# A macaron transformer layer on one core: x in four column chunks between the first weight blocks, and ten unread matmuls at the head of TensorE's program

## What is computed

```python
def _rmsnorm(x, g):
    y = xf * lax.rsqrt(jnp.mean(xf * xf, axis=-1, keepdims=True) + EPS)
    return y * g
x = x + 0.5 * _swiglu(_rmsnorm(x, ffn1_norm[l]), w_gate, w_up, w_down)   # D_FF = 5632
```

## Time and profile before

| | us |
|---|---|
| median of three runs | 2510.61 |
| lowest and highest run | 2506.28 and 2514.45 |
| span of the profiled execution | 2504.7 |
| busy in that span: PE, PEld | 2453.5, 2389.8 |
| busy in that span: DVE, ACT, POOL | 1186.1, 801.0, 138.6 |

### The profile page before, as it was taken

One profiled execution on the slowest core, in us unless ns is written; L12 is line 12 of the kernel. 1 busy time (PEld: TensorE's weight loads), 2 busy tenths in 40 slices (PEclk: granted clock), 3 DMA queues, 4 the chain that ended last, 5 costly groups with the idle time before them and its releaser, 6 DMA issues.

```text
span 2504.7 us, 36768 instructions
## 1 busy us (share of the span) xinstructions
PE 2453.5 (98%) x16307; PEld 2389.8 (95%) x16307; DVE 1186.1 (47%) x892; ACT 801.0 (32%) x686; POOL 138.6 (6%) x59
## 2 busy tenths in 40 slices
PE   7999999999999999999999989999999999999998
PEld 5999999999999999989899669999999999999998
DVE  6444444444444447345484226444444444444445
ACT  3322322232323224333333224323322332233223
POOL 2000000000000001000000001000000000000001
PEclk9999999999999999999999899999999999999999
DMA  5444444444444444515153113444444444444441
GB/s 193 152 152 151 151 150 145 145 147 149 150 151 151 151 150 152 162 62 179 55 151 119 42 43 118 152 152 151 150 145 147 146 150 150 151 151 151 151 147 64
DMA packets 178896, 345.98 MB, mean 138 GB/s; under 512 B 10383, under 2 KB 17046, under 8 KB 178518
## 3 DMA queue, kind: packets, MB, share of 16 engines
q1 hardware_dynamic: 175942, 337.11, 41.8%
q0 software_dynamic: 2160, 7.60, 0.9%
q10 hardware_dynamic: 736, 0.41, 0.1%
HBM read 339.45 MB, written 5.65 MB: 138 GB/s over the span
## 4 chain that ended last, share of the span: by engine, by line
PE 95%; DVE 3%; ACT 1%; DMA 0%; issue 0%; SPq 0%; DVEq 0%; ACTq 0%
PE ps L1202 29%; PE ps L1203 29%; PE ps L1204 29%; DVE mov_lo L822 2%; DVE w_lo L805 1%; PE ps L1554 1%; PE ps L1553 1%; PE ps L1383 1%; PE ps L1381 0%; DMA work<-in_x_sample 0%; PE ps L1278 0%; PE ps L1564 0%; PE ps L1412 0%; PE ps L1579 0%; PE ps L1428 0%; PE ps L1238 0%
## 5 line engine op out<-in xcount | busy, mean ns | idle before, releaser
L1202 PE MATMUL ps<-mov_hi,w_hi 128*128 128x320 f32 x3568 | 1108.3, 311 | 9.6 <-DVE w_lo L805 8.6
L1203 PE MATMUL ps<-mov_lo,w_hi 128*128 128x320 f32 x3568 | 1104.4, 310 | 0.0
L1204 PE MATMUL ps<-mov_hi,w_lo 128*128 128x320 f32 x3568 | 1104.2, 309 | 0.0
L805 DVE TENSOR_TENSOR w_lo<-raw,w_hi 128x2048 fp32r<-128x2048 f32 x313 | 717.3, 2292 | 744.7 <-ACT w_hi L499 744.6
L499 ACT CAST w_hi<-raw 128x2048 fp32r<-128x2048 f32 x313 | 596.8, 1907 | 1429.0 <-PE ps L1204 1428.9
L1202 PEld LDWEIGHTS ps<-mov_hi,w_hi 128*128 128x128 f32 x3568 | 671.7, 188 | 12.7 <-issue 10.3
L1203 PEld LDWEIGHTS ps<-mov_lo,w_hi 128*128 128x128 f32 x3568 | 671.6, 188 | 0.5
L1204 PEld LDWEIGHTS ps<-mov_hi,w_lo 128*128 128x128 f32 x3568 | 671.5, 188 | 0.0
L1202 PE MATMUL ps<-h_hi,w_hi 128*128 128x320 f32 x1488 | 462.9, 311 | 4.7 <-DVE h_lo L894 4.7
L1203 PE MATMUL ps<-h_lo,w_hi 128*128 128x320 f32 x1488 | 462.4, 311 | 0.0
L1204 PE MATMUL ps<-h_hi,w_lo 128*128 128x320 f32 x1488 | 462.3, 311 | 0.0
(11 more groups left out here) (193 smaller groups left out, 835.9 us busy)
## 6 DMA issues: line engine op xcount, KB each, us to landing
raw<-in_ffn_w_gate SPq DMA_DIRECT2D x88, 1024.0 KB, 5.2
raw<-in_ffn_w_up SPq DMA_DIRECT2D x88, 1024.0 KB, 5.2
raw<-in_ffn_w_down SPq DMA_DIRECT2D x88, 1024.0 KB, 5.1
raw<-in_w_in SPq DMA_DIRECT2D x28, 1024.0 KB, 5.3
raw<-in_w_out SPq DMA_DIRECT2D x16, 1024.0 KB, 5.1
raw<-in_mla_w_uq SPq DMA_DIRECT2D x12, 256.0 KB, 4.2
raw<-in_w_in SPq DMA_DIRECT2D x4, 640.0 KB, 4.1
work<-in_x_prompt SPq DMA_DIRECT2D x2, 1024.0 KB, 6.4
```

The lines of the kernel that those rows point to most:

```text
L805: dve.tensor_tensor(w_lo[:, n % SPLIT_SLOTS, :], raw[:, n % RAW_SLOTS, :], w_hi[:, n % SPLIT_SLOTS, :].bitcast(F32), ALU.subtract).then_in ...
L1202: pe.matmul(out, w[0], x[0], start=first, stop=False)
L1203: pe.matmul(out, w[0], x[1], start=False, stop=False)
L1204: return pe.matmul(out, w[1], x[0], start=False, stop=last)
```

## The change

SP loads x in four chunks of 512 columns, chunk 0 first, and the others each ahead of one of the gate blocks 1 to 3; gate block 0 comes in four quarters with a semaphore each. The gains are now loaded by ACT's queue and the lambdas by POOL's. PE's program begins with ten matmuls of the tile of ones, whose result nobody reads; then it turns the gains and lambdas, then x tiles 0 to 3, and goes to unit 0. Tiles 4 to 7, 8 to 11 and 12 to 15 are turned in the middle of units 0, 1 and 2. All x tiles go through banks 4 to 7. Unit 0 runs with its four row tiles as the outer loop, each started when its part of `mov_lo` and its quarter of `w_lo` are there.

ACT makes `mov_hi` and DVE `mov_lo` straight from PSUM, and DVE copies the tile to `xT` after that. POOL's squares, the additions and PE's sum for the first block are gone. In their place ACT squares x in its token layout with a running sum along the row (`sum_x`, three instructions), mean, root, reciprocal and the Newton step are made on 128 x 3 elements (`x_norm`), and in the middle of unit 3 PE spreads the factors over the partitions with three matmuls (`spread_rstd`); DVE copies the result to `rstd` (`x_spread_out`). The load of the rest of the table moves behind the first up loads. Semaphore counts of the later norms are renumbered to match.

The diff without new semaphores, renumbered counts and context:

```diff
-        x_in = [sem(f"x_in{i}") for i in range(3)]
+        x_in = [sem(f"x_in{q}") for q in range(4)]
+        first_in = [sem(f"first_in{k}") for k in range(UK - 1)]
...
-            return j if j < 4 else 4 + j % 4
+            return 4 + j % 4
...
-            for t, (r0, rows) in enumerate(TOK):
-                src = x_prompt[0, r0:r0 + rows, :] if t < 2 else x_sample[0]
-                sp.dma_start(wk(X_TOK + t * D, D, slice(0, rows)), src).then_inc(x_in[t], 16)
-            for col, g, n in ((G_F1, ffn1_norm[0], KT), (G_MIX, mix_norm[0], KT), (G_F2, ffn2_norm[0], KT),
-                              (G_FIN, final_norm, KT), (G_SUB, da_subln[0], 1), (G_Q, q_norm[0], 4),
-                              (G_KV, kv_norm[0], 2)):
-                sp.dma_start(wk(S_ROWS, P, slice(col, col + n)),
-                              g.rearrange("(j p) -> j p", p=P)).then_inc(gains_in, 16)
-            for c, v in enumerate((lq1, lq2, lk1, lk2)):
-                sp.dma_start(wk(S_LROWS, HALF, slice(c, c + 1)), v).then_inc(lam_in, 16)
+            def x_load(q):
+                cols = slice(UC * q, UC * q + UC)
+                for t, (r0, rows) in enumerate(TOK):
+                    src = x_prompt[0, r0:r0 + rows, cols] if t < 2 else x_sample[0, :, cols]
+                    sp.dma_start(wk(X_TOK + t * D + UC * q, UC, slice(0, rows)), src).then_inc(x_in[q], 16)
             def ffn_loads(u0, gate, up, down):
+                if u0 == 0:
+                    x_load(0)
+                    for k in range(UK):
+                        sp.dma_start(raw[:, 0, UC * k:UC * k + UC], gate[0, P * k:P * k + P, 0:UC]
+                                     ).then_inc(first_in[k] if k < UK - 1 else raw_in[0], 16)
+                    for q in range(1, 4):
+                        x_load(q)
+                        load(q, 0, block_of(gate, UC * q, 0))
+                else:
+                    for q in range(4):
+                        load(u0 + q, 0, block_of(gate, UC * q, 0))
                 for q in range(4):
-                    load(u0 + q, 0, block_of(gate, UC * q, 0))
+                    load(u0 + 4 + q, 0, block_of(up, UC * q, 0))
                 if u0 == 0:
                     sp.dma_start(tab[:, C_STACK:C_ALL], table[:, C_STACK:C_ALL]).then_inc(tab_in, 16)
-                for q in range(4):
-                    load(u0 + 4 + q, 0, block_of(up, UC * q, 0))
                 with sp.Fori(0, PARTS - 1) as i:
...
             pool.memset(ones[:, :], 1.0).then_inc(ones_set, 1)
+            for c, v in enumerate((lq1, lq2, lk1, lk2)):
+                pool.dma_start(wk(S_LROWS, HALF, slice(c, c + 1)), v).then_inc(lam_in, 16)
...
-            pool.wait_ge(x_copied, 4)
-            pool.tensor_tensor(wk3(F_ACC, 4, T), xT[:, 0:4, :], xT[:, 0:4, :], ALU.mult).then_inc(squared, 1)
-            pool.wait_ge(x_copied, 8)
-            pool.tensor_tensor(wk3(F_SQ, 4, T), xT[:, 4:8, :], xT[:, 4:8, :], ALU.mult).then_inc(squared, 1)
-            add_squares(0)
...
-                    if f == 0 and j < 2:
-                        first_moving_hi(2 + j)
-                        square(0, 2 + j)
+                    if f == 0 and j < 3:
+                        first_moving_hi(j + 1)
+                        sum_x(j)
                     if j == 2:
-                        root(2 * f)
+                        root(2) if f else x_roots()
...
+            for col, g, n in ((G_F1, ffn1_norm[0], KT), (G_MIX, mix_norm[0], KT), (G_F2, ffn2_norm[0], KT),
+                              (G_FIN, final_norm, KT), (G_SUB, da_subln[0], 1), (G_Q, q_norm[0], 4),
+                              (G_KV, kv_norm[0], 2)):
+                act.dma_start(wk(S_ROWS, P, slice(col, col + n)),
+                              g.rearrange("(j p) -> j p", p=P)).then_inc(gains_in, 16)
+            def x_tile_hi(j):
+                act.wait_ge(x_turned, j + 1)
+                act.activation(mov_hi[:, j, :], ps[:, x_bank(j), 0:T], ACT.Copy,
+                               scale=gains[:, G_F1 + j:G_F1 + j + 1]).then_inc(x_hi, 1)
+            def first_moving_hi(q):
+                for j in range(4 * q, 4 * q + 4):
+                    x_tile_hi(j)
+            def sum_x(t):
+                rows = TOK[t][1]
+                if t == 0:
+                    act.wait_ge(tok_set, 1)
+                    for q in range(4):
+                        act.wait_ge(x_in[q], 16 * 3)
+                else:
+                    act.wait_ge(x_sums, t)
+                act.activation(wk(F_SQ, D, slice(0, rows)), wk(X_TOK + t * D, D, slice(0, rows)), ACT.Square,
+                               accum_out=xs[0:rows, t:t + 1]).then_inc(x_sums, 1)
+            def x_roots():
+                act.wait_ge(x_mean, 1)
+                act.activation(xs[:, 3:6], xs[:, 0:3], ACT.Sqrt).then_inc(x_root, 1)
             act.wait_ge(gains_set, 1)
-            def first_moving_hi(q):
-                act.wait_ge(x_copied, 4 * q + 4)
-                moving_hi(0, q, G_F1)
-            first_moving_hi(0)
-            hi(0)
-            first_moving_hi(1)
+            for k in range(UK):
+                x_tile_hi(k)
+                act.wait_ge(first_in[k] if k < UK - 1 else raw_in[0], 16)
+                act.copy(w_hi[:, 0, UC * k:UC * k + UC],
+                         raw[:, 0, UC * k:UC * k + UC]).then_inc(first_hi if k < UK - 1 else hi_done, 1)
...
-                    if f == 0 and j < 2:
-                        moving_lo(0, 2 + j, G_F1)
-                    if f == 0 and j == 0:
-                        copy_x(3)
+                    if f == 0 and j < 3:
+                        x_tiles_lo(j + 1)
                     if j == 2:
-                        norm(2 * f, 4 * ((g0 + 1) % 2))
+                        norm(2, 4 * ((g0 + 1) % 2)) if f else x_norm()
                     if j == 3:
+                        if f == 0:
+                            x_spread_out()
                         drain_gate(u0 + 3, 0, g0)
...
+            dve.memset(xs[:, :], 1.0)
             dve.memset(tok[:, :], 1.0).then_inc(tok_set, 1)
-            def copy_x(q):
+            def x_tile_lo(j):
+                dve.wait_ge(x_hi, j + 1)
+                dve.scalar_tensor_tensor(mov_lo[:, j, :], ps[:, x_bank(j), 0:T], gains[:, G_F1 + j:G_F1 + j + 1],
+                                         mov_hi[:, j, :].bitcast(F32), ALU.mult, ALU.subtract).then_inc(x_lo, 1)
+            def copy_x(j):
+                dve.tensor_copy(xT[:, j, :], ps[:, x_bank(j), 0:T]).then_inc(x_copied, 1)
+            def x_tiles_lo(q):
                 for j in range(4 * q, 4 * q + 4):
-                    dve.wait_ge(x_turned, j + 1)
-                    dve.tensor_copy(xT[:, j, :], ps[:, x_bank(j), 0:T]).then_inc(x_copied, 1)
-            copy_x(0)
+                    x_tile_lo(j)
+                    copy_x(j)
+            def x_norm():
+                dve.wait_ge(x_sums, 3)
+                dve.tensor_scalar(xs[:, 0:3], xs[:, 0:3], 1.0 / D, EPS, ALU.mult, ALU.add).then_inc(x_mean, 1)
+                dve.wait_ge(x_root, 1)
+                y, a, v = xs[:, 3:6], xs[:, 6:9], xs[:, 0:3]
+                link(dve.reciprocal(y, y))
+                link(dve.tensor_tensor(a, y, y, ALU.mult))
+                link(dve.tensor_tensor(a, a, v, ALU.mult))
+                link(dve.tensor_scalar(a, a, -0.5, 1.5, ALU.mult, ALU.add))
+                link(dve.tensor_tensor(a, a, y, ALU.mult))
+                dve.wait_ge(ones_set, 1)
+                for t, (r0, rows) in enumerate(TOK):
+                    last = dve.tensor_scalar(wk(F_ACC + P * t, P, slice(0, rows)), ones[0:rows, :],
+                                             xs[0:rows, 6 + t:7 + t], None, ALU.mult)
+                last.then_inc(x_rstd, 1)
+            def x_spread_out():
+                dve.wait_ge(x_spread, 1)
+                dve.tensor_copy(rstd[:, :], ps[:, 4, 0:T]).then_inc(x_rstd, 1)
+                dve.wait_ge(x_rstd, 2)
             dve.wait_ge(gains_turned, 1)
-            dve.tensor_copy(gains[:, :], ps[:, 7, 0:G_ALL]).then_inc(gains_set, 1)
-            dve.tensor_copy(lamin[:, 0:4], ps[0:HALF, 7, 128:132]).then_inc(gains_set, 1)
-            copy_x(1)
-            moving_lo(0, 0, G_F1)
-            lo(0)
-            copy_x(2)
-            moving_lo(0, 1, G_F1)
+            dve.tensor_copy(gains[:, :], ps[:, 0, 0:G_ALL]).then_inc(gains_set, 1)
+            dve.tensor_copy(lamin[:, 0:4], ps[0:HALF, 0, 128:132]).then_inc(gains_set, 1)
+            dve.wait_ge(gains_set, 1)
+            for k in range(UK):
+                x_tile_lo(k)
+                dve.wait_ge(first_hi if k < UK - 1 else hi_done, k + 1 if k < UK - 1 else 1)
+                cols = slice(UC * k, UC * k + UC)
+                dve.tensor_tensor(w_lo[:, 0, cols], raw[:, 0, cols], w_hi[:, 0, cols].bitcast(F32),
+                                  ALU.subtract).then_inc(first_lo if k < UK - 1 else lo_done, 1)
+            for j in range(4):
+                copy_x(j)
...
```

(71 more changed lines are left out.)

36 lines of the change are left out of this document (20 added, 16 removed).

## The result

The changed kernel took 2491.73 us (median of 11 runs, 2483.86 to 2497.02), the one before 2507.05 (11 runs beside them, 2499.82 to 2518.93): ratio 0.993, interval 0.9913 to 0.9946. The forecast was 2494.7, in a range of 2488 to 2503. The span fell from 2504.7 to 2489.7 us, by 15.0. The time of a run on record is its span and 2.4 to 3.8 us more in the kernel before, 1.9 to 2.2 in the changed one.

What follows compares the result with a forecast made beforehand. TensorE (PE), busy 98% of the span, was taken as the bound, with gain only before unit 4. Its start moving from 64.13 to 48.2 took 15.9 us off span 2504.7, giving 2488.8; plus 5.9, 2494.7 us, range 2488 to 2503.

Steps and rivals of the forecast that it cites:

- Small rows in at 7.0: At the start: gain and lambda loads, on ACT's and POOL's queues, landed by 7.0 us, at the earliest 5.7, latest 11.
- Rival 2: At the start: the small rows land at 11 us, as before the change; time 2498.7 us; chance 10%.
- Unit 0 at 11.3, bound by PE's turn: Unit 0 starts at 11.3 us instead of 29.59, after PE's turns; the ACT and DVE chain ends at 10.7.
- Unit 0 lasts 10.8: Unit 0 takes 10.8 us as before, with a turn and some 13 slow matmuls, ending at 22.1.
- Units 1 and 2 at 9.25, unit 3 at 7.65: Units 1 and 2 hold a turn each, 9.25 us; unit 3 swaps summing for three matmuls, 7.65 us.
- T4 = 48.2: Start of unit 4, the first up-projection unit: 48.2 us in the changed kernel instead of 64.13.
- DVE's chain 0.8 us ahead of PE at unit 1: In unit 0: DVE's splits, tiles and copies end at 21.3 us, 0.8 us before PE is done.
- Rival 3: Units 0 to 2: DVE's chain outlasts PE's unit at the dear tile price, some 3 us thrice; 2503.5 us; chance 8%.
- x all in at 18 to 19, where ACT needs it at 19.1: Last x chunk lands at about 18 to 19 us, when ACT's first row sum comes to it, 19.1.
- Rivals 1 and 5: Units 0 to 3: clock falls in each turn, 2499.5 us, 12%; or stays at 1.2 GHz until unit 4, 2520.8 us, 4%.
- rival 4: Behind the earlier start: something later, such as a wait in the first loop turn, gives it back; no change; chance 6%.
- 5.9 us from span to time: Whole kernel: the runs' median, 2510.61 us, lies 5.9 above the execution's span; carried over to the changed kernel.

Runs made afterwards that it cites:

- e10: The changed kernel again, unaltered, as a check on how well it repeats: 2494.14 us, ratio 0.9937 to the kernel before.
- e7: Changed kernel with a tiny unread activation on ACT ahead of its wait for the gains, loading the function table early: 2487.74 us, single run.
- e1: Changed kernel without its ten dummy matmuls: 2492.49 us, ratio 0.9945 to the kernel before.
- e4: Changed kernel with eleven useless multiplications of a scratch tile on POOL, from the first turned tile on: 2492.15 us, single run.
- e6: Changed kernel with 22 dummy matmuls at the head instead of 10, and ten more behind the first turn: 2484.77 us, single run.
- e8: Changed kernel with the edits of e5, e6 and e7 together: 2489.48 us, single run.
- e11: e8 with step 0's x tiles ahead of block 1's split, row sums one step later, and 16 and 2 dummies: 2489.29 us, ratio 0.9932 to kernel before.
- e3: Kernel before the change, with the squares of x tiles 0 to 7 made by ACT instead of POOL: 2499.54 us, single run.
- e2: Changed kernel with all four x chunks loaded ahead of the first weight block: 2500.64 us, single run.
- e5: Changed kernel with the lambdas turned in unit 3, so PE's start waits for the gains alone: 2494.87 us, single run.

## Why the prediction held, and where it was off

The mechanism was right: the whole change acts up to unit 4, the PE chain is unbroken from unit 0 on, and the sign and the size are about as forecast. Point by point, by the prediction's steps:

- **Chunk 0 near 5 us, the last weight quarter near 8:** the numbers given there (2 us, then 704 and 1728 KB at 418 KB per us) make 3.7 and 6.1. Nothing hung on it: neither PE nor ACT waited for either.
- **Small rows in at 7.0:** 7.46, in e10 6.97. Rival 2 (11 us) is out. That the separate queues are the reason was not tried; the rows landed with the stream at 387 GB/s in the slice from 7 to 8 us.
- **Unit 0 at 11.3, bound by PE's turn:** 12.34, and bound by the other chain, which I had at 10.7. This step failed. I had let ACT load its table as soon as the gains were there. In the trace the load starts at 9.09, when the first turned tile is released; it stands behind that wait. On this chain the load costs 0.9 us, the small rows 0.5 and the first pieces of ACT and DVE 0.3, together the 1.6 from 10.7 to 12.34. e7 moves the load away, which takes 1.3 us off the first `mov_hi` tile.
- **Unit 0 lasts 10.8:** 11.9. The slow beginning had 20 matmuls at 0.27 us, where the kernel before had 12 (I had put it at 13), 1.0 us more. In e1 it had 12, in e10 18; how many it is hangs on when the clock rises, which no step of mine could give.
- **Units 1 and 2 at 9.25, unit 3 at 7.65:** 9.37 twice and 8.0. Together 0.6 us; the summing is six records in 0.81 us where I had 0.54.
- **T4 = 48.2:** 1.0 + 1.1 + 0.2 + 0.4 = 2.7 later; measured 51.02.
- **DVE's chain 0.8 us ahead of PE at unit 1:** its eighth `mov_lo` ends at 22.7, unit 1 starts near 24.2. The prices 0.48 and 0.65 were 0.55 and 0.68. Rival 3 was ruled out for half of its reason: e4 shows that even with POOL busy these tiles would have kept the low price, and the splits would not.
- **x all in at 18 to 19, where ACT needs it at 19.1:** 22.82, and ACT waited 1.57 us (timeline: 22.82, row sum, released by x). I had taken the full rate of 418 GB/s; the slices above show 223 to 389. It was hidden by 1.5 us or so of slack in unit 1, and where the start is better (e6, e8) it is the bound. Of all misses this is the one that mattered most for further edits.
- **The norm of x ready 1.6 us before PE asks:** ready at 45.1, asked for at 46.66, 1.5 us.
- **Dummies cost nothing and bring nothing:** e1, and the clock's 0.50 in the slice from 9 to 10 us. In e10 they did not even raise it.
- **Rivals 1 and 5, the clock falls in a turn:** not in a turn that stands between matmuls. Those behind the turns of 18.54, 27.91 and 37.28 us are 0.15 apart, in e6 and e11 also those behind the first. In e7 the clock fell at 9.8 us, but there a wait of 1.62 us stood ahead of the turn. The Trainium skill, "TensorE: Matmul & The Clock Gate", Part 4, says that transposes don't count as a busy PE in the same way; the trace agrees in that the kernel before ran 36 turning matmuls from 11.9 to 23.8 us, all at the low pace, without raising the clock. Turns of 2.14 us amid matmuls kept the high clock, and no run shows what a longer stretch of them would do to it.
- **Nothing given back later (rival 4):** PE's idle time behind 64 us is the same. The span lost 15.0 us, close to the forecast 15.9, but this agreement is partly luck: 13.1 us come from the change and the rest from the clock behind the start in this execution.
- **5.9 us from span to time:** this step failed. 5.9 was the median of three runs less the span of one execution; as its own time is 2.4 to 3.8 us above its span in the runs on record, the rest was scatter between runs. Afterwards it is 2.0 (2491.73 and 2489.7, the same execution). The span was forecast at 2488.8, 0.9 too low, the time at 2494.7, 3.0 too high: the late unit 4 (2.8), the help of the clock (1.9) and this constant (3.9) add up to that.

Where the 12.6 us at the drain come from is shown in part: 4.55 by taking POOL off DVE's path, measured on the kernel before (e3), and 3.1 by the order of x and weights, measured on the changed one (e2). That the two add up is not shown. What is then left, some 5 us, I put down to starting on a quarter of x, the small rows on separate queues and the first block in quarters; none of these was tried alone.

Open: why a given gap of PE lowers the clock in one execution and not in another (14 to 44 us at the low clock behind the start in the profiles of this study, the last microseconds of the kernel left out), and whether work that keeps PE busy in its gaps, most of them between 1390 and 1510 us, would pay. By the line of 0.38 us per us it is worth at most 5 to 17 us, an estimate, as much as this whole change, and it was not tried.

## What to carry to other kernels

When a start is rebuilt, write down for each engine what stands ahead of its first piece of work in program order, one-off costs such as ACT's table load included, and see which of them sits behind a wait that it doesn't need. A gain at the head goes as far as the next unhidden transfer or row sum: check the slack of each later unit before adding edits up (e5, e6 and e7 together had no earlier drain than e7 alone). Where a difference of a few us is in question, compare a marker inside the trace, not medians alone, and take the time at the low clock from the trace of the same stretch: the mean clock of a run leaves out what lies ahead of the first recorded change. Before a gain of a microsecond is put down to an edit, see whether the clock was the same in both.

## What was not expected of the hardware

- Whether DVE is held up by a POOL tensor operation that runs when it starts depends on where its operands lie: 128x512 with both in SBUF 0.68 us alone and 2.35 beside POOL; 128x320 with one in PSUM 0.55 both ways; 128x320 times four with both in SBUF 1.93 and 6.54. Where DVE had started first it was POOL that took longer, 4.89 us instead of 2.94 (e3, seen once).
- The table load (1.28 us) starts only when the wait of the activation behind it is over (9.09 us after, 16.23 before), and e7's unread activation takes it out of the way.
- Small rows of 0.2 to 8 KB took 3.5 to 4.5 us from the last issue to landing while x streamed in, though on queues of their own.
- The run-to-run scatter of this kernel's span, 2496 to 2518 us, is mostly the time TensorE spends at 1.2 GHz: 0.38 us of span per us, correlation 0.95 over 42 runs. A PE gap of 2.35 us lowered the clock behind it in 8 of 13 executions, for 3.4 us, in which PE was busy throughout.
- Ten fp32 matmuls of 128 columns from 1 us on raised the clock during their 4.0 us in one execution of the kernel and not in another, where they took 4.6.
